# A hybrid attention and convolution layer: mixing of the dilation groups issued in three pieces, its loads ahead of the next chunk's, first two tiles of the output product's left operand split ahead of the last merge

## The chip, the core and the metric

The kernel runs on one core of a Trainium2 chip. Its engines have queues of their own and meet at semaphores: TensorE (PE in the profile, its weight loads PEld), VectorE (DVE), ScalarE (ACT), GpSimd (POOL) and SyncE (SP, which here only issues loads). The metric is the device time of one execution in microseconds, the median over several.

## What is computed

One decoder layer over 2048 tokens and 1024 features, in f32. Cut to what matters here:

```python
proj = h @ w_in + b_in                       # q, k, v | z_attn | u_x, g_b, g_c | z_conv | g_A, g_B
for g, (window, dilation) in enumerate(((128, 1), (512, 4), (2048, 16))):
    o_g, lse_g = dilated_window_attention(q_g, k_g, v_g, window, dilation)
mix_w  = softmax(stack(lse_g), axis=groups)
o_attn = sum over g of mix_w[g] * o_g        # 4 heads of 64: 256 wide
y_attn = (o_attn * silu(z_attn)) @ w_proj_attn
y_conv = (g_b * conv3(g_c * u_x) * silu(z_conv)) @ w_proj_conv
m      = sigmoid(g_A) * y_attn + sigmoid(g_B) * y_conv
x      = layer_norm(alpha * x + gate * (m @ w_out + b_out))
```

Every product of two f32 matrices is made of three: each operand is split into a rounded part (`hi`) and the rest (`lo`), and hi·hi, hi·lo and lo·hi are summed.

## The kernel before

**The input products.** `h @ w_in` is done in 68 groups of two 128-wide tiles of columns over 1024 tokens. A group is done with seven half-size products instead of eight (Strassen), so there are 476 products (`NS`), and `product(n)` works on piece p = n mod 7 of group g = n // 7. One product is 12 matmuls of 128x128 by 512 (lines 1035, 1037, 1038). Four of a group's seven go to the bank `acc[:, g % 2]`, so p = 6 can only start when the result of p = 4 has been taken out of that bank (semaphore `c22_out`). For a group of gates ScalarE takes p = 0, 1, 2 and 6 and VectorE takes p = 3, 4 and 5 (`take_gate`, rows `room<-acc,part`). The gates, made in halves of the tokens, are the last groups of this phase.

**The order on each engine is written out by hand.** Every engine's program is a loop over slots m, one slot for a product. In slot m VectorE takes the result of product m-1 (if p is 3 to 5), then forms the sums of weight tiles for coming products (`combine`, rows `s_tmp<-...` and `w_raw<-w_raw`), then splits the weights of product m+3 (`split_w`, rows `w_lo<-...`), then does whatever else is due in that slot. An engine does its work strictly in that order, and a wait holds all that stands behind it.

**Mixing.** `mix(u)` makes one 128 x 512 piece of `o_attn * silu(z_attn)`: u = 2·chunk + p, for four chunks of 512 tokens and two halves p of the width. For each dilation group dg it waits for that group's data (`mixa_in[dg]`) and multiplies by the weights, for dg 1 and 2 it adds to the first; then one multiplication with `z`, one cast (line 1775) and one subtraction: six multiplications and additions, a cast and a subtraction, all 128x512. `mix(0)` and `mix(1)` stand in slots 452 and 462 of the products (`MIX_AT = NS-24, NS-14`); the other six stand in the merge loop. `load_mix(u, dg)` on SP loads the data of one group: one load of `att_d` (line 681; for dg 2 in runs of 32 elements, 128 bytes) and two of `wg_d` (line 684), for dg 0 also one of `za_d`.

**The merge loop.** After the products come 32 units n = 8·chunk + i, one 128-wide tile of m each. TensorE does `project_att(n)` (6 matmuls, lines 1141 to 1143) and `project_conv(n)` (24 matmuls, lines 1161 to 1163). VectorE does `gate_att(n)` (first gate times attention), in the first chunk `split_wp(n+2)` (rest of a weight tile of `w_proj_conv`, which ScalarE has rounded in `round_wp`, line 1351), at i = 2 and 5 `mix` for the next chunk, at i = 4 and 6 `split_b` (rest of the next chunk's half kh of the convolution's output), and last `merge(n)` (second gate times convolution, then the sum), whose result goes to `mix_d`. SP's part of this loop: `load_merge(n+2)` (the two gates, line 703), at i = 0 `load_b(chunk+1, 0)` and `load_b(chunk+1, 1)` (1 MB each, line 715), at i = 0 and 3 the three groups of a `load_mix`. ScalarE rounds `b` at i = 3 and 5 (`round_b`, line 1347), in the first chunk between the `round_wp`.

**The output product.** Last come 16 tiles of 128 tokens, 48 matmuls each (lines 1203 to 1205). `load_m` brings a tile of m back, `round_m` (ScalarE, line 1437) rounds it and `split_m` (VectorE) makes its rest. TensorE waits for that split (`m_lo_done`), for tile 0 also for the merges of unit 29 and before, for tile 1 for all 32. VectorE's small operations are recorded under line 1459 whatever they do, so its rows are told apart by their tiles.

Of the kernel before, what the change touches and what calls it, by code (L numbers as in the profile page):

```python
# [8 lines left out]
ALU = mybir.AluOpType  # L9
# [156 lines left out]
def build(nc, x, c, w_ada, b_ada, w_in, b_in, conv_w, w_pa, w_pc, w_out, b_out, ln_g, ln_b, out):  # L166
# [23 lines left out]
    with ExitStack() as top:  # L190
# [357 lines left out]
        with nc.Block() as block:  # L548
            @block.sync
            def _(sp):  # L550
# [227 lines left out]
                for n in range(NMU):  # L778
                    chunk, i = unit(n)
                    if n + 2 < NMU:  # L780
                        load_merge(n + 2)
                    if i == 0 and chunk < 3:
                        for kh in range(2):
                            load_b(chunk + 1, kh)
                    for p in range(KA):
                        if i == 3 * p and chunk < 3:
                            for dg in range(3):
                                load_mix(KA * (chunk + 1) + p, dg)
                    for b in range(4):
                        if n == 3 * KT + (0, 1, 3, 5)[b]:  # L790
                            load_wo(b)
                    if n == 3 * KT + 2:
                        load_m(0)
                        load_m(1)
                    if n == 3 * KT + 4:
                        load_xr(0)
                        load_xr(1)
                        load_xr(2)
                        sp.wait_ge(ada_out, 16)
                        sp.dma_start(gb, b_out.broadcast_to([P, D])).then_inc(bc_in, 16)  # L800
                        sp.dma_start(xr[:, 3], ada_d.broadcast_to([P, D])).then_inc(bc_in, 16)
# [650 lines left out]
            def _(dve):  # L1452
# [297 lines left out]
                    dve.wait_ge(pa_rounded, k + 1)  # L1750
                    tt_op(pa_lo[:, k], pa_raw[:, k], pa_hi[:, k].bitcast(F32), ALU.subtract).then_inc(pa_split, 1)

                def mix(u):
                    tc, p = u // KA, u % KA
                    o = mix_a[:, 0]
                    for dg in range(3):
                        a, w = mix_a[:, dg], mix_w[:, dg]
                        dve.wait_ge(mixa_in[dg], 48 * (u + 1))
                        if dg == 0:
                            own_t.up(tt_op(o, a, w, ALU.mult))  # L1760
                            own_t.wait()
                        else:
                            own_t.up(tt_op(by_token(w, dg), natural(a, dg), by_token(w, dg), ALU.mult))
                            own_t.wait()
                            own_t.up(tt_op(o, o, w, ALU.add))
                            own_t.wait()
                    dve.wait_ge(za_in, 16 * (u + 1))
                    own_t.up(tt_op(o, o, mix_z, ALU.mult))
                    own_t.wait()
                    if p == 0 and tc >= 2:  # L1770
                        dve.wait_ge(ya_done, KT * (tc - 1))
                    if p == 0 and tc == 1:
                        for r in range(3):
                            dve.wait_ge(gt_out[r], 16 * gate_stores(r))
                    own_t.up(nc.vector.tensor_copy(o_hi[tc % 2][:, p], o))
                    own_t.wait()
                    tt_op(o_lo[tc % 2][:, p], o, o_hi[tc % 2][:, p].bitcast(F32), ALU.subtract).then_inc(mix_done, 1)
# [44 lines left out]
                for m in range(NS + 2):  # L1822
                    if m and m <= NS:
                        g, p = at(m - 1)
                        kind = PLAN[g].kind
                        if p >= 3:
                            dve.wait_ge(prod, m)
                            if p < 6:
                                dve.wait_ge(sums(g, p)[3], g + 1)
                        if kind in "qkv" and 3 <= p < 6:  # L1830
                            take_rows(g, p)
                        if kind == "ug" and p >= 3:
                            take_ug(g, p)
                        if kind == "gz" and p >= 3:
                            take_gz(g, p)
                        if kind == "za" and p >= 3:
                            take_za(g, p)
                        if kind == "gate" and 3 <= p < 6:
                            take_gate(g, p)
                    if m - 1 in ATT_AT[:NSTEP]:  # L1840
                        bias_max(ATT_AT.index(m - 1))
                    if m - 2 in ATT_AT[2:]:
                        take_o(ATT_AT.index(m - 2) - 2)
                    for n, when in enumerate((-4, -3, -2, 0)):
                        if (m - when) % NP == 0 and (m - when) // NP < NG and (n == 3 or m - when):
                            combine((m - when) // NP, n)
                    if m + 3 < NS:
                        split_w(m + 3)
                    if m < 4:
                        if m == 1:  # L1850
                            dve.wait_ge(t1_ready, 1)
                            tt_op(hs[:, 1], hs[:, 2], hs[:, 1], ALU.subtract).then_inc(t1_ready, 1)
                        if m == 3:
                            dve.wait_ge(dumped["b21"], 16)
                            dve.wait_ge(t1_ready, 2)
                            dve.wait_ge(h_ready, 16)
                            tt_op(hs[:, 3], hs[:, 3], hs[:, 0], ALU.subtract).then_inc(t1_ready, 1)
                        first_t_lo(m + 3)
                    for ph in range(1, 3):
                        for p in range(NP):  # L1860
                            if m == FIRST[ph] + T_LO_AT[p]:
                                split_t(ph, p)
                    if m >= 3 and m - 3 < NS:
                        g, p = at(m - 3)
                        if PLAN[g].kind == "za" and 3 <= p < 6:
                            weigh_za(g, p - 3)
                        if PLAN[g].kind == "ug" and p == 6:
                            taps(g)
                    if m - 2 in TURN_AT:
                        pieces(TURN_AT.index(m - 2))  # L1870
                    for k in range(KT):
                        if m == BG2 + 2 * k + 2:
                            gate_row(k)
                        if m == BG2 + 26 + 2 * k + 2:
                            scale_wo(k)
                    for half in range(2):
                        if m == SUM_AT[half] + 1:
                            gate_sum(half)
                    if m == STAT + 1:
                        copy_stats()  # L1880
                    if m == WEIGH:
                        weigh_groups(0)
                    if m == WEIGH + 4:
                        weigh_groups(1)
                    for k in range(KA):
                        if m == PA_AT + 2 * k + 1:
                            split_pa(k)
                    for u in range(KA):
                        if m == MIX_AT[u]:
                            mix(u)  # L1890
                    for kh in range(2):
                        if m == NS - 2 + kh:
                            split_b(0, kh)
                    for i in range(2):
                        if m == NS + i:
                            split_wp(i)
                for n in range(NMU):
                    c, i = unit(n)
                    gate_att(n)
                    if n + 2 < KT:  # L1900
                        split_wp(n + 2)
                    for kh in range(2):
                        if c < 3 and i == 4 + 2 * kh:
                            split_b(c + 1, kh)
                    for p in range(KA):
                        if c < 3 and i == 2 + 3 * p:
                            mix(KA * (c + 1) + p)
                    for b in range(4):
                        if n == 3 * KT + (2, 3, 5, 7)[b]:
                            split_wo(b)  # L1910
                    merge(n)

                def split_m(tt):
                    r = tt % 2
                    dve.wait_ge(m_hi_done, tt + 1)
                    tt_op(m_part(t_lo, r), m_raw(r), m_part(t_hi, r).bitcast(F32), ALU.subtract).then_inc(m_lo_done, 1)

                split_m(0)
                split_m(1)
                own_t.up(nc.vector.memset(eps[:], LN_EPS))  # L1920
                dve.wait_ge(bc_in, 64)
                own_t.up(tt_op(gb, gb, xr[:, 3], ALU.mult))
# [57 lines left out]
```

## Time and profile before

| | us |
|---|---|
| median of 3 runs | 1983.62 |
| lowest and highest | 1981.62, 1984.23 |
| the profiled execution | 1979.5 |
| its span, first to last instruction | 1977.7 |
| TensorE busy in it | 1907.7 (96%) |
| VectorE busy | 1227.0 (62%) |
| ScalarE busy | 860.7 (44%) |

The span is the time between the first and the last instruction; 1.8 us of the execution lie around it. Busy time of an engine says how much it did, not whether anyone waited for it. A row of the timeline gives an engine's operation with its start and length and, in brackets, how long the engine sat idle before it and what ended that. A row with x6 stands for six operations in one go. The granted clock of TensorE is 1.00 at full speed.

### The profile page before, as it was taken

Reading aid. Unit: us, or ns where it says so; the run is one execution under the profiler, and the core shown is the slowest. Engines: PE = TensorE matmul, PEld = TensorE weight load, DVE = VectorE, ACT = ScalarE, POOL = GpSimd, SP = SyncE. Lnnn points to the kernel's source line nnn. Section 1 sums busy time; section 2 is a strip of 40 time slices with the busy share of each in tenths; the row PEclk is TensorE's granted clock in tenths of the full one; section 3 lists DMA queues with packets and bytes.
Section 4 is the critical chain, followed back from the end, with each engine's and each line's share of the span. In section 5 each row is a group of like instructions: output and inputs, shape, how many; then the busy total and the mean of one; then the engine's idle time right before and its main releaser. Section 6 shows DMA issues by size and latency. Waiting matters only on the chain. (4 is left out here: it accounts for less than half of the span.)

```text
span 1977.7 us, 25526 instructions
## 1 busy us (share of the span) xinstructions
PE 1907.7 (96%) x8989; PEld 1517.6 (77%) x8989; DVE 1227.0 (62%) x2171; ACT 860.7 (44%) x1513; POOL 199.3 (10%) x354
## 2 busy tenths in 40 slices
PE   3799999999999999999989999999999999999998
PEld 3588888877777777777767777777787878887886
DVE  5655564446666666665657666666655665555776
ACT  2544543344545454666665455544553510012222
POOL 0012210120000000011210000000011100000000
PEclk9799999999999999999999999999999999999999
DMA  8566653342323222264762322323255688883442
GB/s 310 188 201 196 205 181 116 96 124 81 97 73 92 80 78 79 85 203 149 257 252 86 96 85 80 92 80 106 81 152 151 210 232 229 243 277 124 149 142 92
DMA packets 303789, 289.03 MB, mean 146 GB/s; under 512 B 38356, under 2 KB 255568, under 8 KB 299952
## 3 DMA queue, kind: packets, MB, share of 16 engines
q1 hardware_dynamic: 277712, 200.06, 35.0%
q0 software_dynamic: 25952, 87.35, 12.2%
q8 instruction: 73, 1.20, 0.3%
q14 instruction: 52, 0.43, 0.1%
HBM read 198.97 MB, written 88.38 MB: 145 GB/s over the span
## 5 line engine op out<-in xcount | busy, mean ns | idle before, releaser
L1035 PE MATMUL acc<-t_hi,w_hi 128*128 128x512 f32 x1904 | 761.0, 400 | 23.6 <-DVE room L1459 13.1
L1038 PE MATMUL acc<-t_hi,w_lo 128*128 128x512 f32 x1904 | 744.7, 391 | 0.0
L1037 PE MATMUL acc<-t_lo,w_hi 128*128 128x512 f32 x1904 | 743.9, 391 | 0.0
L1035 PEld LDWEIGHTS acc<-t_hi,w_hi 128*128 128x128 f32 x1904 | 358.6, 188 | 121.8 <-issue 40.1
L1038 PEld LDWEIGHTS acc<-t_hi,w_lo 128*128 128x128 f32 x1904 | 358.8, 188 | 77.7
L1037 PEld LDWEIGHTS acc<-t_lo,w_hi 128*128 128x128 f32 x1904 | 359.3, 189 | 71.3 <-issue 0.5
L1459 DVE TENSOR_TENSOR room<-acc,part 128x512 f32<-128x512 f32 x204 | 140.8, 690 | 216.9 <-PE acc L1038 215.2
L1459 DVE TENSOR_TENSOR room<-room 128x512 f32<-128x512 f32 (+3 forms) x224 | 178.7, 802 | 98.1 <-DMA room<-wg_d 39.5
L1263 ACT ACTIVATE part<-acc,cols 128x512 f32<-128x512 f32 x204 | 140.1, 687 | 222.3 <-PE acc L1038 221.7
L1459 DVE TENSOR_TENSOR w_lo<-w_raw,w_hi 128x512 fp32r<-128x512 f32 x272 | 184.6, 686 | 60.1 <-ACT w_hi L1245 60.1
L1245 ACT CAST w_hi<-w_raw 128x512 fp32r<-128x512 f32 x272 | 167.5, 616 | 89.5 <-PE acc L1038 87.9
L1245 ACT CAST w_hi<-s_tmp 128x512 fp32r<-128x512 f32 x204 | 126.2, 619 | 144.9 <-PE acc L1038 138.9
L1459 DVE TENSOR_TENSOR w_lo<-s_tmp,w_hi 128x512 fp32r<-128x512 f32 x204 | 140.0, 686 | 65.6 <-ACT w_hi L1245 64.0
L1678 DVE CUSTOM_DVE_ANT_0 room<-score,room 128x128 f32<-128x128 f32 (+1 forms) x192 | 62.5, 363 | 108.9 <-PE score L1073 108.1
L900 POOL DMA_DIRECT2D att_d<-room x96 | 51.7, 539 | 734.2 <-DVE room L1688 726.0
L1339 ACT COPY room<-pt_o 128x256 f32<-128x256 f32 (+1 forms) x96 | 47.2, 491 | 134.1 <-PE pt_o L1082 133.0
L1203 PE MATMUL acc<-t_hi 128*128 128x512 f32 x256 | 99.7, 389 | 2.6 <-DVE t_lo L1459 2.6
L1204 PE MATMUL acc<-t_lo,t_hi 128*128 128x512 f32 x256 | 99.6, 389 | 0.0
L1205 PE MATMUL acc<-t_hi,t_lo 128*128 128x512 f32 x256 | 99.6, 389 | 0.0
L1330 ACT ACTIVATE room<-room 128x128 f32<-128x128 f32 (+1 forms) x192 | 87.0, 454 | 22.5 <-DVE room L1682 22.0
L1161 PE MATMUL acc<-t_hi 128*128 128x512 f32 x192 | 74.9, 390 | 2.3 <-DVE t_lo L1459 2.3
L1162 PE MATMUL acc<-t_lo,t_hi 128*128 128x512 f32 x192 | 74.7, 389 | 0.0
(205 smaller groups left out, 2024.2 us busy)
## 6 DMA issues: line engine op xcount, KB each, us to landing
w_raw<-in_w_in SPq DMA_DIRECT2D x136, 512.0 KB, 5.2
gate_d<-room POOLq DMA_DIRECT2D x64, 256.0 KB, 2.8
w_raw<-gate_d SPq DMA_DIRECT2D x32, 512.0 KB, 5.2
qk_d<-room POOLq DMA_DIRECT2D x24, 512.0 KB, 4.1
room<-qk_d SPq DMA_DIRECT2D x192, 64.0 KB, 2.1
ada_w<-in_w_ada SPq DMA_DIRECT2D x8, 1024.0 KB, 12.1
room<-in_x SPq DMA_DIRECT2D x32, 256.0 KB, 6.4
t_raw<-tr_d SPq DMA_DIRECT2D x8, 1024.0 KB, 8.1
```

What stands on the lines that cost most here:

```text
L1035: nc.tensor.matmul(to, w_hi[:, s, k], t_hi[:, p, k], start=(first and k == 0), stop=False, skip_group_check=True)
L1037: nc.tensor.matmul(to, w_hi[:, s, k], t_lo[:, p, k], start=False, stop=False, skip_group_check=True)
L1038: mm = nc.tensor.matmul(to, w_lo[:, s, k], t_hi[:, p, k], start=False, stop=(last and k == KH - 1), skip_group_check=True)
L1161: nc.tensor.matmul(to, w_h[:, k], b_h, start=(k == 0), stop=False)
L1162: nc.tensor.matmul(to, w_h[:, k], b_l, start=False, stop=False)
L1203: nc.tensor.matmul(to, m_h[:, k], wo_hi[:, k, w], start=(k == 0), stop=False)
L1204: nc.tensor.matmul(to, m_h[:, k], wo_lo[:, k, w], start=False, stop=False)
L1205: mm = nc.tensor.matmul(to, m_l[:, k], wo_hi[:, k, w], start=False, stop=(k == KT - 1))
L1245: nc.scalar.copy(w_hi[:, n % RING], src).then_inc(hi_done, 1)
L1263: ins = nc.scalar.activation(to, src, ACT.Identity, bias=col(gr.tb if p == 1 else gr.ta))
L1330: ex = nc.scalar.activation(prob[:, h, 0:w], prob[:, h, 0:w], ACT.Exp, bias=all_m[:, t, h, blk:blk + 1], scale=SCALE, accum_out=all_d[:, t ...
L1459: return nc.vector.tensor_tensor(o, a, b, op)
```

## The change

Three things are moved; no operation is added or removed.

1. `mix(0)` and `mix(1)`, so far one block each in one slot, are issued in three pieces, one dilation group in each of three slots in a row (`MIX_AT[u] + dg`). The last piece also has the multiplication with `z`, the cast and the subtraction. The six mixes of the merge loop stay whole.
2. In SP's part of the merge loop the loads of the mix (i = 0) are issued ahead of the two loads of the next chunk's `b`.
3. `split_m(0)` and `split_m(1)` on VectorE, so far behind `merge(31)`, stand ahead of it.

```diff
                     if n + 2 < NMU:
                         load_merge(n + 2)
-                    if i == 0 and chunk < 3:
-                        for kh in range(2):
-                            load_b(chunk + 1, kh)
                     for p in range(KA):
                         if i == 3 * p and chunk < 3:
                             for dg in range(3):
                                 load_mix(KA * (chunk + 1) + p, dg)
+                    if i == 0 and chunk < 3:
+                        for kh in range(2):
+                            load_b(chunk + 1, kh)
...
-                def mix(u):
+                def mix(u, dgs=(0, 1, 2)):
                     tc, p = u // KA, u % KA
                     o = mix_a[:, 0]
-                    for dg in range(3):
+                    for dg in dgs:
...
+                    if dgs[-1] < 2:
+                        return
                     dve.wait_ge(za_in, 16 * (u + 1))
...
                     for u in range(KA):
-                        if m == MIX_AT[u]:
-                            mix(u)
+
+                        for dg in range(3):
+                            if m == MIX_AT[u] + dg:
+                                mix(u, (dg,))
...
                             split_wo(b)
+                    if n == NMU - 1:
+                        split_m(0)
+                        split_m(1)
                     merge(n)
...
-                split_m(0)
-                split_m(1)
```

On VectorE, slots 452 to 455 of the products. `room<-acc,part` takes a product out of its bank, `room<-room` is the mix. Before:

```order
L1459 TENSOR_TENSOR room<-acc,part 128x512
L1459 TENSOR_TENSOR s_tmp<-s_tmp,w_raw 128x512
L1459 TENSOR_TENSOR w_lo<-w_raw,w_hi 128x512
L1459 TENSOR_TENSOR room<-room 128x512 x6
L1775 CAST o_hi_a<-room 128x512
L1459 TENSOR_TENSOR o_lo_a<-room,o_hi_a 128x512
L1459 TENSOR_TENSOR room<-acc,part 128x512
L1459 TENSOR_TENSOR w_raw<-w_raw 128x512
```

The same slots now:

```order
L1459 TENSOR_TENSOR room<-acc,part 128x512
L1459 TENSOR_TENSOR s_tmp<-s_tmp,w_raw 128x512
L1459 TENSOR_TENSOR w_lo<-w_raw,w_hi 128x512
L1459 TENSOR_TENSOR room<-room 128x512
L1459 TENSOR_TENSOR room<-acc,part 128x512
L1459 TENSOR_TENSOR w_raw<-w_raw 128x512
L1459 TENSOR_TENSOR w_lo<-s_tmp,w_hi 128x512
L1459 TENSOR_TENSOR room<-room 128x512 x2
L1459 TENSOR_TENSOR room<-acc,part 128x512
L1459 TENSOR_TENSOR w_lo<-s_tmp,w_hi 128x512
L1459 TENSOR_TENSOR room<-room 128x512 x3
L1777 CAST o_hi_a<-room 128x512
```

The take of slot 453 (the second `room<-acc,part`) had eight operations of the mix ahead of it and now has one.

On SP, unit 0 of the merge loop (`conv_d` is the next chunk's `b`; `att_d`, `wg_d` and `za_d` are the mix's data):

```order
+L681 DMA room<-att_d 128x4x128
+L684 DMA room<-wg_d 64x512 x2
+L688 DMA room<-za_d 128x512
+L681 DMA room<-att_d 128x4x128
+L684 DMA room<-wg_d 64x512 x2
+L681 DMA room<-att_d 128x16x32
+L684 DMA room<-wg_d 64x512 x2
 L715 DMA t_raw<-conv_d 128x4x512
 L715 DMA wl_raw<-conv_d 128x4x512
-L681 DMA room<-att_d 128x4x128
-L684 DMA room<-wg_d 64x512 x2
-L688 DMA room<-za_d 128x512
```

Ten loads of the mix went from behind the two of `b` to ahead of them; the gates' loads of unit 3 and later (line 703) follow both, as before.

On VectorE, the end of the merge loop (`w_raw<-acc,w_raw` and `w_raw<-w_raw` are `merge(31)`, `s_tmp` and `part` hold tiles 0 and 1 of m):

```order
-L1459 TENSOR_TENSOR w_raw<-acc,w_raw 128x512
-L1459 TENSOR_TENSOR w_raw<-w_raw 128x512
 L1459 TENSOR_TENSOR t_lo<-s_tmp,t_hi 128x1024
 L1459 TENSOR_TENSOR t_lo<-part,t_hi 128x1024
-L1920 MEMSET eps 128x1
+L1459 TENSOR_TENSOR w_raw<-acc,w_raw 128x512
+L1459 TENSOR_TENSOR w_raw<-w_raw 128x512
+L1925 MEMSET eps 128x1
```

The two splits no longer stand behind the merge of unit 31, which waits for TensorE's last product of the loop.

## Rows read from the trace of the kernel before

**Rows 1.** The page's first part: busy time, share, instructions of each engine.

```profile
PE 1907.7 (96%) x8989; PEld 1517.6 (77%) x8989; DVE 1227.0 (62%) x2171; ACT 860.7 (44%) x1513; POOL 199.3 (10%) x354
```

**Rows 2.** Waits of TensorE: line, waited for, total us, times, longest.

```profile
PE acc L1203 <- DVE t_lo L1459: 2.6, 1, 2.6
PE acc L1161 <- DVE t_lo L1459: 2.3, 2, 1.7
```

**Rows 3.** Timeline, VectorE and TensorE at mix(0): start, length, operation, [idle before].

```profile
1502.44 5.13 DVE L1459 TENSOR_TENSOR room<-room 128x512 f32<-128x512 f32 x6
...
1505.40 0.39 PE L1038 MATMUL acc<-t_hi,w_lo 128*128 128x512 f32 x1
...
1508.67 0.68 DVE L1459 TENSOR_TENSOR room<-acc,part 128x512 f32<-128x512 f32 x1
...
1509.50 0.47 PE L1035 MATMUL acc<-t_hi,w_hi 128*128 128x512 f32 x1 [3.71 <-DVE room L1459]
```

**Rows 4.** Windows behind that rest: PE, PEld, DVE, ACT, POOL busy, then PEclk.

```profile
1510.27:1513.65 3.38, 3.38 (x10) 2.63 (x9) 1.82 (x3) 0.00 (x0) 0.54 (x1) 0.50 0.20 78
```

**Rows 5.** Timeline, TensorE: where full speed is back.

```profile
1513.92 0.40 PE L1035 MATMUL acc<-t_hi,w_hi 128*128 128x512 f32 x1
```

**Rows 6.** Timeline, TensorE, units 0 to 5 of the merge loop.

```profile
1573.20 0.50 PE L1161 MATMUL acc<-t_hi 128*128 128x512 f32 x1 [0.60 <-DVE t_lo L1459]
...
1607.11 0.39 PE L1143 MATMUL score<-o_hi_a,pa_lo 128*128 128x512 f32 x1
1609.24 0.50 PE L1161 MATMUL acc<-t_hi 128*128 128x512 f32 x1 [1.74 <-DVE t_lo L1459]
```

**Rows 7.** Timeline, VectorE: mix(2) in unit 2, then unit 3.

```profile
1596.21 0.69 DVE L1459 TENSOR_TENSOR room<-room 128x512 f32<-128x512 f32 x1 [7.18 <-DMA room<-wg_d]
1599.19 1.82 DVE L1459 TENSOR_TENSOR room<-room 128x512 f32<-128x512 f32 x2 [2.29 <-DMA room<-wg_d]
...
1606.04 0.68 DVE L1459 TENSOR_TENSOR w_raw<-acc,w_raw 128x512 f32<-128x512 f32 x1
...
1607.37 0.68 DVE L1459 TENSOR_TENSOR w_raw<-xb,w_raw 128x512 f32<-128x512 f32 x1
1607.97 1.22 DVE L1459 TENSOR_TENSOR t_lo<-t_raw,t_hi 128x1024 fp32r<-128x1024 f32 x1
```

**Rows 8.** Timeline, SP's queue, unit 0 of the merge loop: issue start, length.

```profile
1581.01 0.41 SPq L715 DMA_DIRECT2D t_raw<-conv_d  x1
...
1591.53 7.84 SPq L684 DMA_DIRECT2D room<-wg_d  x2
1599.41 8.42 SPq L703 DMA_DIRECT2D w_raw<-gate_d  x3
```

**Rows 9.** One line's loads, issue to landing: first of b (L715).

```profile
DMA to landing us min/median/max: 5.8/8.9/12.9
```

**Rows 10.** The same of the gates' loads (L703).

```profile
DMA to landing us min/median/max: 3.8/5.2/8.6
```

**Rows 11.** Timeline, ScalarE: rounding of b's first half and of tiles 5 and 6.

```profile
1589.25 1.91 ACT L1347 CAST t_hi<-t_raw 128x2048 fp32r<-128x2048 f32 x1 [10.13 <-DMA t_raw<-conv_d]
1591.06 1.99 ACT L1351 CAST t_hi<-t_raw 128x1024 fp32r<-128x1024 f32 x2
```

**Rows 12.** Timeline, ScalarE, TensorE and VectorE at the merge loop's end.

```profile
1785.06 1.05 ACT L1437 CAST t_hi<-part 128x1024 fp32r<-128x1024 f32 x1
...
1787.05 2.28 DVE L1459 TENSOR_TENSOR t_lo<-t_raw,t_hi 128x2048 fp32r<-128x2048 f32 x1
...
1791.38 0.39 PE L1163 MATMUL acc<-w_hi,t_lo 128*128 128x512 f32 x1
1791.81 0.69 DVE L1459 TENSOR_TENSOR w_raw<-acc,w_raw 128x512 f32<-128x512 f32 x1 [2.48 <-PE acc L1163]
...
1793.14 1.22 DVE L1459 TENSOR_TENSOR t_lo<-s_tmp,t_hi 128x1024 fp32r<-128x1024 f32 x1
...
1794.42 0.50 PE L1203 MATMUL acc<-t_hi 128*128 128x512 f32 x1 [2.65 <-DVE t_lo L1459]
```

More of the change, by code:

```diff
@@ L1896, in _, with split_m @@
                             split_wp(i)
+                def split_m(tt):
+                    r = tt % 2
+                    dve.wait_ge(m_hi_done, tt + 1)
+                    tt_op(m_part(t_lo, r), m_raw(r), m_part(t_hi, r).bitcast(F32), ALU.subtract).then_inc(m_lo_done, 1)
                 for n in range(NMU):
@@ L1910, in _ @@
                             split_wo(b)
+                    if n == NMU - 1:
+                        split_m(0)
+                        split_m(1)
                     merge(n)
[L1913 to L1916, printed above, removed]
-                split_m(0)
-                split_m(1)
                 own_t.up(nc.vector.memset(eps[:], LN_EPS))
```

## The prediction

> **What bounds the kernel now.** TensorE does. The page's busy shares say so first: it is busy for 1907.7 of the 1977.7 us, VectorE for 62% [rows 1]. So only two things can make the kernel faster: fewer or shorter matmuls, and the change touches none, or fewer rests of TensorE. I therefore read next who TensorE waits for, and then the timeline at each rest behind 1500 us, where the change acts. There are four. Two stand in the waits under lines 1161 and 1203 with VectorE's splits as what ended them [rows 2], of which line 1161 has two; the fourth stands in the middle of the last products, and a take out of a bank ended it [rows 3]. The measure for a rest is the distance from the last start before it to the first behind it, less one ordinary step. That step comes from units 0 to 5: 150 starts (24, then four times 30, then 6) from 1573.20 to 1607.11, 33.91 / 149 = 0.227 us [rows 6].
>
> **Part 1, mix(0) and mix(1) in three pieces.** Before, VectorE enters mix(0) at 1502.44 and comes to the take of the next product at 1508.67: 6.23 us in one block [rows 3]. That product's bank is wanted by p = 6 of the same group. TensorE has started its last ready matmul at 1505.40 and goes on at 1509.50 [rows 3]. The clock then adds to it: from 1510.27 to 1513.65 the granted clock is 0.50, the 1.2 GHz level, after it had been 1.00 through the busy stretch before the rest; from 1513.92 the rows have their usual length again [rows 4, 5]. From the start at 1505.40 to that at 1513.92 there are 8.52 us and 13 steps (to three starts ahead of 1510.27, nine in the slow window, which one more matmul reaches into, and the last); at 0.227 they would take 2.95. This rest and its slow stretch cost 5.57 us.
>
> What is there in its place? One piece is one multiplication, about 0.7 us (the first row of mix(2) has 0.69), the second a multiplication and an addition, 1.82 us [rows 7]; the third is what is left of the block, 6.23 - 0.69 - 1.82 = 3.7 us. In the new order I walk VectorE on: piece 0 from 1502.44 to 1503.1; the product that is to be taken ended at about 1503.1 (12 steps of 0.227, or 2.72, ahead of the end of the next at 1505.8), so the take ends at 1503.9, about 1.9 us before TensorE wants the bank. Then a sum of weights and a split (0.7 each, as all 128x512 operations here) to 1505.2, piece 1 to 1507.0, take and split to 1508.5, piece 2 to 1512.2, then the two operations of slot 455 to 1513.6. The first that is late next would be that split, for product 458, which TensorE starts at 1505.8 + 4 x 2.72 = 16.7, so 3.1 us to spare; and the take of p = 5 (done at 1507.8) is wanted only by the second product of the next group at 1511.2. So the new waits behind the pieces are covered by TensorE's own run, and were the cover gone each us of it would be a us of TensorE. Of mix(1) the change can give back nothing: it stands at p = 0 to 2, where VectorE has no take to do, and no rest there is among TensorE's waits. It costs nothing for the same reason. mix(1)'s data can only be asked for when mix(0) is done, now some 3.5 us later, but that load stands in SP's queue six slots (16 us) behind slot 452. Term: **-5.6 us**, between -5.6 and -3.9 (the 4.10 - 0.23 of the rest alone, if the slow clock comes anyway); the second rival has what a new rest would leave of it.
>
> The trace shows the slow clock behind the rest of 4.10 us and none behind those of 2.13 and 3.04 us, where the step is the usual one at once. The Trainium skill ("TensorE: Matmul & The Clock Gate", Part 1: The HAM clock gate) says that a gate halves the clock once the array has been idle long enough and frees it after sustained work; by that rule the slow stretch goes with the rest that brought it, which gives -5.6 for this term, and without it the sum would have -3.9. The trace agrees as far as one slow stretch can show it.
>
> **Part 2, loads of the mix ahead of those of b.** TensorE stands from 1607.11 to 1609.24 before unit 5's convolution, 2.13 - 0.23 = **1.9 us**, waiting for the rest of weight tile 5 [rows 6]. VectorE makes it at 1607.97, behind mix(2), merge(2) (1606.04) and the gate of unit 3 (1607.37); and mix(2) was late because its data came late: 7.18 and 2.29 us idle before its first two pieces [rows 7]. SP issued b's two loads, 2 MB, at 1581.01, and the mix's behind them [rows 8]. In the new order the mix's first data have no b ahead. How much earlier? Nearest rows: the first of b, issued at 1581.01, lands 8.2 us later by its row's place (ScalarE takes it up at 1589.25 [rows 11]); a load issued there now is the mix's, so VectorE, which comes to mix(2) at about 1589.0 (1596.21 - 7.18), would find dg 0 at 1590 to 1592 rather than 1596.2, and mix(2) ends 4 to 6 us earlier. That is more than the 1.9 that is missing.
>
> But the gates' load of unit 3 stays last in line. It was issued at 1599.41, after a 7.84 us issue of two small `wg_d` loads behind the 128-byte runs of dg 2 [rows 8]; SP has the same issues to do in the new order, so I leave it at 1599.4 at the latest. By its row such a load takes 3.8 to 8.6 us, median 5.2 [rows 10], so it lands at 1603.2 to 1608.0, and now b's 2 MB stand right ahead of it. The chain behind it, gate of unit 3 and split of tile 5, is 1607.97 + 1.22 - 1607.37 = 1.82 us [rows 7]; TensorE wants it at 1607.34. So the rest goes wholly if the gates land by 1605.5, which the median does (1604.6). Term: -1.9 us, between -1.9 and +0.7 (landing at 1608.0: 1609.8 against 1609.2). I take -1.9 since the median is on that side and SP may well be there earlier.
>
> On that: the rows say that the queue stalls for 7.2 to 7.8 us where 128-byte runs are in it. The Trainium skill ("DMA: Bandwidth & Descriptors", Why small descriptors are slow (HBM only)) gives small descriptors a fixed cost each; it speaks against the new order, since all of b and the gates of unit 3 now stand behind such a load. By it the second term would be about 0 and the whole sum -8.4.
>
> b itself now lands later: issued at up to 1598.3 instead of 1581, 5.8 to 12.9 us to landing [rows 9], so 1604 to 1611. Its own use is far off (unit 8, at 1573.2 + 8 x 6.8 = 1628). What stands behind it on ScalarE is the rounding of weight tiles 6 and 7; this is the new wait and a rival below. In chunks 1 and 2 the same exchange takes place; there VectorE idles for the mix's data but TensorE has no rest, and ScalarE has no weight tiles behind b: nothing.
>
> **Part 3, the two splits ahead of merge(31).** TensorE starts its last matmul of the loop at 1791.38 and the first of the output product at 1794.42: 3.04 - 0.23 = **2.8 us**. VectorE idles 2.48 us, until 1791.81, for TensorE's end, does the merge's two operations, and only then, at 1793.14, the split that TensorE waits for [rows 12]. Its inputs had been rounded by 1786.11 (1785.06 + 1.05 for the second). In the new order VectorE is free at 1789.33 (1787.05 + 2.28); two splits at 1.2 bring it to 1791.7, still before it can merge, and TensorE goes on without a rest: tile 0 wants only the merges up to unit 29, and tile 1 comes 48 steps, 10.9 us, later. The splits lie wholly in VectorE's idle 2.48 us; without that cover the merge alone would be later, which is 10 us from being wanted. Term: -2.8 us; if the splits came only behind TensorE's end all the same, just the merge's two operations would go from ahead of them, 1793.14 - 1791.81 = 1.3 us, the other end., lower bound -2.3 should the merge's bank still be waited for in some way that I don't see.
>
> The fourth rest, 0.99 us before 1573.20, stays: nothing of its chain is moved.
>
> **Sum.** -5.6 - 1.9 - 2.8 = -10.3 us. On the profiled execution 1979.5 becomes 1969.2. That execution was 4.1 us below the median of the runs shown, 1983.62, and the rests are a matter of order, not of that offset: 1983.6 - 10.3 = **1973.3 us**.
>
> **The rivals.**
> First, the second rest stays because the gates of unit 3 now come last behind b: -8.4, or **1975.2**. For it: 2 MB more right ahead of them; against: the median landing and a shorter stall when SP's queue starts the mix without b in it. As low as -7.7 if they land at 1608.0.
>
> Second, the pieces don't free TensorE: a take or split behind piece 2, the longest, is late for a product, and the first rest comes back in part, 1.5 to 4 us of the 5.6, with or without the slow clock. Against it are the 1.9 and 3.1 us to spare worked out above; for it, that ScalarE's rounding of slot 456 waits for a sum of slot 455 that stands behind piece 2. Sum -4.3 on the mean: **1979.3**, half of it on either side of 1979.7.
>
> Third, slower: b's first half now comes late to ScalarE, which waits for it in unit 3 and rounds tile 6 only then. From its landing T it is 1.91 + 1.0 + 1.22 + some 0.2 = 4.3 us until TensorE may start unit 6's convolution [rows 7, 11], which it wants at 1607.34 + 6.8 = 1614.1. TensorE stands as soon as T is beyond 1609.8, and everything gained is lost beyond T = 1620.1. The latest by the rows is 1611.2, a rest of 1.4 us; to be slower by 0.2% it would have to be 1624, with a load of 26 us where the longest was 12.9. Price then some 15 us of rest: **1988**.
>
> **How the numbers follow.** Forecast 0.58, first rival 0.27, second 0.12, third 0.03. A measurement of this kernel can tell about 0.2%, 4 us, from no change, so faster means below 1979.7: 0.58 + 0.27 and half of 0.12 is 0.91, of which I leave 0.01 to no change for the runs' own spread of 2.6 us: 0.90. Same: 0.07. Slower: 0.03. Range: downward the forecast less 1.5 us for the medians' spread and less the 0.99 us rest, should it go too, and a little over: 1970.0. Upward the first rival (1975.2) with the clock's 1.7 us not gained and 1.5 us of spread, 1978.4; the other end of the third term lies in it too. That leaves out most of the second and the third.
>
> **What would show it.** Right: TensorE's waits have no row with the take `room` behind 1500 us and none at line 1203; PEclk has no 0.5 in the last products; mix(2)'s first piece starts at about 1591 less 5.6, and TensorE's last matmul before the output product and the first of it are 0.23 us apart. Wrong in part 2: a rest under line 1161 with VectorE's split, VectorE idle for `gate_d` before it. The second rival: a rest in line 1035 ended by `w_lo` or `room` within 15 us of slot 452. The third: a rest under line 1161 of over 3 us while ScalarE waits for `conv_d`. The whole would be wrong if TensorE were slower at its own matmuls, a step other than 0.227.

## The result and the profile after

| | before | changed |
|---|---|---|
| median, us | 1981.61 (6 runs) | 1968.04 (6 runs) |
| lowest and highest | 1981.24, 1984.23 | 1967.17, 1970.05 |
| profiled execution | 1979.5 | 1967.78 |
| its span | 1977.7 | 1965.9 |

The ratio is 0.9931, with a 95% interval from 0.9919 to 0.9942: 13.6 us faster, between 11.5 and 16.1. The forecast was 10.3 us faster and 1973.3, with a range from 1970.0: the direction was right and each of the three rests went, the gain was a third larger, and the time fell out of the range by 2 us.

TensorE's waits in the changed kernel, the lines that answer to [rows 2] (waited for, total us, times, longest):

```profile
PE acc L1035 <- DVE room L1459: 9.4, 3, 5.5
...
PE acc L1161 <- DVE t_lo L1459: 0.6, 1, 0.6
```

There is no row of line 1203 any more, line 1161 has kept only the rest of 0.6 us that the prediction left alone, and of the four waits for `room` that line 1035 had before (13.1 us together), the one of 3.7 us is gone. The windows around the three places (columns as in [rows 4]):

```profile
1490.00:1510.00 20.00, 20.00 (x90) 16.57 (x89) 12.86 (x19) 10.10 (x17) 2.43 (x5) 1.00 0.35 112
1590.00:1610.00 20.00, 20.00 (x90) 16.57 (x89) 15.44 (x19) 5.62 (x4) 1.62 (x3) 1.00 1.06 283
1775.00:1795.00 20.00, 20.00 (x90) 16.57 (x89) 11.30 (x12) 3.46 (x4) 1.08 (x2) 1.00 0.55 158
```

TensorE is busy for all of each 20 us, at a granted clock of 1.00, where before there were rests and a stretch at 0.50.

VectorE at the pieces of mix(0), which answers to [rows 3] (timeline):

```profile
1501.31 0.69 DVE L1459 TENSOR_TENSOR room<-room 128x512 f32<-128x512 f32 x1
1502.04 0.69 DVE L1459 TENSOR_TENSOR room<-acc,part 128x512 f32<-128x512 f32 x1
...
1504.08 1.82 DVE L1459 TENSOR_TENSOR room<-room 128x512 f32<-128x512 f32 x2
1505.93 0.69 DVE L1459 TENSOR_TENSOR room<-acc,part 128x512 f32<-128x512 f32 x1
```

The take that TensorE waits for starts 0.73 us behind the start of the mix, not 6.23.

VectorE at mix(2) and unit 3, which answers to [rows 7]:

```profile
1582.22 0.68 DVE L1459 TENSOR_TENSOR room<-room 128x512 f32<-128x512 f32 x1
1584.67 1.81 DVE L1459 TENSOR_TENSOR room<-room 128x512 f32<-128x512 f32 x2 [1.76 <-DMA room<-wg_d]
1588.01 2.56 DVE L1459 TENSOR_TENSOR room<-room 128x512 f32<-128x512 f32 x3 [1.53 <-DMA room<-wg_d]
...
1595.83 0.69 DVE L1459 TENSOR_TENSOR w_raw<-xb,w_raw 128x512 f32<-128x512 f32 x1 [2.73 <-DMA w_raw<-gate_d]
1596.43 1.22 DVE L1459 TENSOR_TENSOR t_lo<-t_raw,t_hi 128x1024 fp32r<-128x1024 f32 x1
```

The first piece no longer waits at all (7.18 us before), and the gates of unit 3 are now what comes last, as the first rival had it: VectorE idles 2.73 us for them. But it is done with the split at 1597.65 and TensorE starts unit 5's convolution at 1600.61, so that wait costs nothing. SP's queue there, which answers to [rows 8]:

```profile
1573.68 0.60 SPq L681 DMA_DIRECT2D room<-att_d  x1
...
1578.94 5.69 SPq L684 DMA_DIRECT2D room<-wg_d  x2
1584.72 1.36 SPq L715 DMA_DIRECT2D t_raw<-conv_d  x1
...
1586.69 6.79 SPq L703 DMA_DIRECT2D w_raw<-gate_d  x3
```

From the first load of the group to the gates' it is 13.0 us, where it was 18.4: the long issue behind the 128-byte runs is 5.69 instead of 7.84, and the shorter ones ahead of it shrank too.

The end of the merge loop, which answers to [rows 12]:

```profile
1780.49 1.22 DVE L1459 TENSOR_TENSOR t_lo<-s_tmp,t_hi 128x1024 fp32r<-128x1024 f32 x1
...
1782.62 0.39 PE L1163 MATMUL acc<-w_hi,t_lo 128*128 128x512 f32 x1
1782.85 0.39 PE L1203 MATMUL acc<-t_hi 128*128 128x512 f32 x1
...
1783.05 0.69 DVE L1459 TENSOR_TENSOR w_raw<-acc,w_raw 128x512 f32<-128x512 f32 x1 [0.21 <-PE acc L1163]
```

The output product starts 0.23 us behind the last start of the loop, one ordinary step, and the two splits lie in what was VectorE's idle time.

**What the two traces leave open.** I matched the starts of TensorE's matmuls in both traces, one by one. The changed kernel gains 5.5 us around mix(0), 2.0 at unit 5 and 2.9 at the output product, 10.4 together, so the sum of 10.3 is right on this pair. It is 1.15 us ahead before the first changed instruction: a wait for a load at 881 us (1.2) is gone. That is no work of the change, since only the first trace of the kernel before has this wait and the twelve others of this study don't. It makes 11.6 of the spans' 11.8. The medians say 13.6. Two theories: (A) the slow clock follows TensorE's rests in some executions and not in others, and the profile of before showed an execution with little of it; (B) the surplus lies elsewhere, in waits for loads.

### The profile page after: what moved, and what is told of

Its sections match the earlier page's. It is cut to its first block, busy times and chain, and to the rows that moved or that the text cites. A ratio compares the mean times of both kernels' runs of the same rounds, so it can differ in the third digit from the quotient of the medians.

```text
span 1965.9 us, 25526 instructions
## 1 busy us (share of the span) xinstructions
PE 1906.4 (97%) x8989; PEld 1518.2 (77%) x8989; DVE 1227.8 (62%) x2171; ACT 860.7 (44%) x1513; POOL 199.3 (10%) x354
## 3 DMA queue, kind: packets, MB, share of 16 engines
q0 software_dynamic: 25952, 87.35, 12.3%
## 4 chain that ended last, share of the span: by engine, by line
PE 92%; DVE 2%; DMA 2%; ACT 2%; issue 1%; SPq 0%; DVEq 0%; ACTq 0%
PE acc L1035 22%; PE acc L1038 21%; PE acc L1037 21%; PE acc L1161 3%; PE acc L1205 3%; PE acc L1163 3%; PE acc L1204 3%; PE acc L1162 3%; PE acc L1203 3%; PE score L1073 3%; PE pt_o L1082 2%; PE xb L1105 2%; DMA ada_w<-in_w_ada 1%; PE xb L1108 1%; DVE room L1459 1%
## 5 line engine op out<-in xcount | busy, mean ns | idle before, releaser
L1204 PE MATMUL acc<-t_lo,t_hi 128*128 128x512 f32 x256 | 99.6, 389 | 0.0
L1205 PE MATMUL acc<-t_hi,t_lo 128*128 128x512 f32 x256 | 99.6, 389 | 0.0
L1163 PE MATMUL acc<-t_hi,t_lo 128*128 128x512 f32 x192 | 74.7, 389 | 0.0
```

What stands on the lines that cost most here:

```text
L1163: mm = nc.tensor.matmul(to, w_l[:, k], b_h, start=False, stop=(k == KT - 1))
L1204: nc.tensor.matmul(to, m_h[:, k], wo_lo[:, k, w], start=False, stop=False)
L1205: mm = nc.tensor.matmul(to, m_l[:, k], wo_hi[:, k, w], start=False, stop=(k == KT - 1))
```

## The experiments

Each was timed in five rounds beside the kernel before, and has a trace. A stretch at half clock was found as steps of 0.427 us between starts of 512-column matmuls, where 0.227 is the ordinary one.

**The kernel before again** (no edit).

> The kernel before, unchanged, for its own spread. In its first profile TensorE had the slow clock behind one of the three rests only (4.10 us) and its profiled execution, 1979.5 us, was faster than all six timed ones (1981.24 to 1984.23). Theory A (the granted clock is what the trace of one execution missed: in most executions one or two more rests bring a slow stretch of 1.6 to 1.7 us each): median 1981 to 1983, and the second profile, if it is 1.6 us or more longer than 1979.5, shows one stretch at 0.50 more. Theory B (executions differ elsewhere, in waits for DMA ahead of 1500 us): the same medians, but a longer profile shows longer waits for loads and the same slow stretches.

Measured: 1981.89 (12 runs, 1977.61 to 1985.56), ratio 1.0003 (0.9992 to 1.0014). The profiled execution took 1977.61, 2 us less than the first profile though it shows a stretch at 0.50 more, behind a rest of 2.9 us at 1025 us that all these kernels have. It had shorter waits for loads, as (B) has it, 1.2 us at 881 and 0.8 at 1274: between two single traces (B) is real. Two windows of that trace (columns as above):

```profile
1026.00:1029.50 3.50, 3.50 (x10) 2.71 (x9) 2.05 (x4) 0.04 (x1) 0.54 (x1) 0.52 1.01 413
1508.50:1510.60 2.10, 2.10 (x6) 1.65 (x5) 1.95 (x4) 0.01 (x1) 0.54 (x1) 0.50 0.32 125
```

The slow stretch behind mix(0) is 2.1 us here and was 3.4 [rows 4]; that behind the rest at 1025 was not there at all in the first trace. So a single trace doesn't tell what a rest costs. Nor does every slow stretch cost time. Behind 1025 us the first trace, without one, has a second rest, ended by a take of ScalarE, and the nine traces with a slow stretch there have 0.8 us of idle or less in its place (the first trace, then the changed kernel's):

```profile
1036.78 0.47 PE L1035 MATMUL acc<-t_hi,w_hi 128*128 128x512 f32 x1 [2.07 <-ACT part L1263]
```

```profile
1035.88 0.47 PE L1035 MATMUL acc<-t_hi,w_hi 128*128 128x512 f32 x1 [0.42 <-ACT part L1263]
```

From 1015 to 1060 us none of the nine loses or gains more than 0.3 us on the first trace: there the slow matmuls only fill time that TensorE would have waited.

With the executions' mean granted clock beside the time, the 69 timed ones of the kernel before (of this and the later calls) fall into

| mean granted clock | executions | median us |
|---|---|---|
| 0.991 | 10 | 1978.2 |
| 0.990 | 23 | 1980.9 |
| 0.989 | 22 | 1982.2 |
| 0.988 | 12 | 1983.4 |
| 0.987 | 2 | 1983.8 |

Half clock for x us lowers the mean by x/2/1980, and takes x/2 us of work away if TensorE is busy all the while, so a step of 0.001 is at most 2.0 us; the table has 5.2 us over three steps. So the clock goes with a good part of this kernel's spread (correlation -0.75), not with all: at 0.990 alone the times reach from 1977.62 to 1983.17.

**Each part alone.** The edits are the three pieces of the diff: the pieces, the order of SP's loads, the place of the splits.

> Only mix(0) and mix(1) in three pieces; loads and last splits as before. Forecast: the rest of 4.10 us in the last products and its slow stretch go, -5.6 us, and the rests before unit 5 (1.9) and before the output product (2.8) stay. Theory A: -5.6 to -6.5. Theory B: -5.6 plus or minus 1. If the pieces alone give -7.5 or more, the surplus of the whole change lies here.

Measured: 1975.03 (6 runs), ratio 0.9969 (0.9958 to 0.9980), 6.1 us faster, between 4.0 and 8.3.

> Only the mix's loads ahead of b's. Forecast: the rest before unit 5 goes, -1.9 us; first rival of the prediction: it stays, 0. Theory A (slow clock behind this rest in many executions of before): -1.9 to -3.6. Theory B: -1.9 plus or minus 1. The trace tells when the gates of unit 3 land and when VectorE comes to the split of tile 5 (before: 1607.97).

Measured: 1977.32 (11 runs), ratio 0.9981 (0.9972 to 0.9989), 3.8 us faster, between 2.2 and 5.5.

> Only the splits of tiles 0 and 1 of m ahead of the last merge. Forecast: the rest before the output product goes, -2.8 us. Theory A (slow clock behind this rest in many executions of before): -2.8 to -4.5. Theory B: -2.8 plus or minus 1.

Measured: 1976.02 (8 runs), ratio 0.9974 (0.9964 to 0.9984), 5.2 us faster, between 3.2 and 7.1.

Each part gains at least its rest, and the three add up to 15.1, which the intervals don't tell from 13.6. The second and third lie above what their rests are worth without the clock (1.9 and 2.8), both with the whole of their intervals. The traces show a reason for the third. With the pieces alone, the two rests that stay both have the slow clock behind them (timeline, then windows around what follows):

```profile
1602.20 0.79 PE L1161 MATMUL acc<-t_hi 128*128 128x512 f32 x1 [2.72 <-DVE t_lo L1459]
```

```profile
1602.50:1605.50 3.00, 3.00 (x8) 2.36 (x8) 2.97 (x5) 0.00 (x0) 0.54 (x1) 0.55 0.92 300
1789.50:1793.00 3.50, 3.50 (x10) 2.69 (x10) 2.71 (x4) 0.00 (x0) 0.00 (x0) 0.51 0.80 202
```

And with the order alone, behind the rest before the output product:

```profile
1789.30:1792.30 3.00, 3.00 (x9) 2.32 (x8) 2.85 (x4) 0.00 (x0) 0.00 (x0) 0.50 0.88 235
```

In the trace of before neither place had it. The first of these rows shows something else: with the pieces alone the rest before unit 5 grew, from 1.74 to 2.72 us of idle. TensorE comes there 8.0 us earlier than before, the split only 7.0, because VectorE's waits for mix(2)'s data grew by 1.0 us (7.87, 2.92 and 1.01 now, 7.18, 2.29 and 1.35 before).

Why the second part gives 3.8 us and not 1.9 stays open. The mean granted clock rose with it (0.9902, where the kernel before had 0.9895 beside it), and the rest before unit 5 differs from execution to execution; but in the three traces of kernels with `mix(0)` in one block in slot 452 and b's loads first, where this rest is not filled, it is 1.5 to 2.1 us long, with no slow stretch behind it. That it is longer in other executions is not shown.

**The rests filled.** The kernel before in its own order; where TensorE rested it now multiplies data that nobody reads, into banks that are free:

```diff
+                def fill(to, count, x):
+                    for _ in range(count):
+                        nc.tensor.matmul(to, x[:, 0:P], x, start=True, stop=True, skip_group_check=True)
...
+                    if n == MIX_AT[0] + 2:
+                        pe.wait_ge(max_ready, NSTEP)
+                        fill(sc_ps[:, 0], 15, t_hi[:, 0, 0])
...
+                    if n == 5:
+                        pe.wait_ge(att_gated, 3)
+                        fill(po[:], 8, t_hi[:, 1, 0])
...
+                    if tt == 0:
+                        pe.wait_ge(att_gated, NMU - 3)
+                        fill(sc_ps[:, 0], 11, t_hi[:, 6, 0])
```

> The kernel before, in its own order, with matmuls that nobody reads put where TensorE rested: 15 of 128x512 (3.4 us) ahead of the product that waits for mix(0), 8 (1.8 us) ahead of unit 5's convolution, 11 (2.5 us) ahead of the output product. The waits last as long as before, so the 8.6 us of rests stay lost. Theory A (the surplus of the change over 10.3 us is slow clock that follows these rests in many executions, not in all): no stretch at 0.50 behind 1400 us in the trace, and 3 to 5 us faster than before. Theory B (the surplus lies elsewhere, in waits for DMA): no faster than before, rather slower by up to 0.5 us per filling that overruns its wait.

Measured: 1977.19 (11 runs), ratio 0.9981 (0.9972 to 0.9990), 3.7 us faster, between 2.0 and 5.5, with 34 matmuls more and every wait as long as before. Its timeline at mix(0) and the window around it:

```profile
1502.77 3.56 PE L1008 MATMUL score<-t_hi 128*128 128x512 f32 x15
1506.59 0.50 PE L1042 MATMUL acc<-t_hi,w_hi 128*128 128x512 f32 x1 [0.26 <-DVE room L1472]
```

```profile
1500.00:1520.00 20.00, 19.74 (x87) 15.98 (x87) 12.95 (x19) 7.84 (x13) 2.16 (x4) 1.00 0.22 75
```

The product starts no sooner than it did (4.04 us between useful starts, 4.10 before; 2.04 and 3.04 at the other two, 2.13 and 3.04 before), yet no stretch at 0.50 is left behind 1400 us while TensorE works, and the mean granted clock of the 11 executions is 0.9918, against 0.9894 of the kernel before. This separates the theories for the medians: idle time taken from TensorE alone, with nothing else moved, gives 3.7 us. That is (A), and (B) gives no reason for it. It also says what the clock is worth here: by the mean clock alone, 0.0024 of 1980 us, it would have been 4.8 us, and 3.7 were measured. Between single traces (B) still counts: of the 4.6 us that this trace is shorter than the first, 2.9 lie ahead of the first filled rest.

**The order's share beside the other two.** The changed kernel with the loads as before.

```diff
-                    for p in range(KA):
-                        if i == 3 * p and chunk < 3:
-                            for dg in range(3):
-                                load_mix(KA * (chunk + 1) + p, dg)
                     if i == 0 and chunk < 3:
                         for kh in range(2):
                             load_b(chunk + 1, kh)
+                    for p in range(KA):
+                        if i == 3 * p and chunk < 3:
+                            for dg in range(3):
+                                load_mix(KA * (chunk + 1) + p, dg)
```

> The changed kernel with the loads in their old order (parts 1 and 3 alone). In the run of part 1 alone the rest before unit 5 had grown from 2.13 to about 3.0 us, because TensorE comes to unit 5 earlier and VectorE, held by loads, does not. So in place of the forecast's 1.9 us the order is worth 2.8 us plus the slow clock that may follow: this kernel 2.8 to 4.5 us slower than the changed one, 1971 to 1972.5; by the forecast's terms alone 1.9 slower, 1970.

Measured: 1971.33 (5 runs, 1967.76 to 1972.10), ratio 0.9949 (0.9937 to 0.9962): 3.3 us slower than the changed kernel's median. The profiled execution is the fastest of them, and its rest before unit 5 is 0.89 us from start to start instead of 2.13 or 3.11:

```profile
1600.58 0.50 PE L1161 MATMUL acc<-t_hi 128*128 128x512 f32 x1 [0.49 <-DVE t_lo L1459]
```

So this rest has no fixed length: here VectorE's waits for mix(2)'s data are 9.6 us together, with the pieces alone they were 11.8. The median fits the expectation, the trace of one execution alone would not have.

**The block in another slot.**

```diff
-MIX_AT = (NS - 24, NS - 14)
+MIX_AT = (NS - 20, NS - 14)
```

> The kernel before with mix(0) still in one block, but in slot 456 instead of 452, where VectorE has no product to take for three slots (as mix(1) has in slot 462). If it is the take behind the block that TensorE waits for, the whole of part 1 is had: no rest there, -5.6 to -6.5 us against before, as e1_pieces. If the length of the block holds up the splits of weights too, a rest of up to 3 us remains under line 1035 behind slot 456.

Measured: 1981.04 (11 runs), ratio 1.0003 (0.9994 to 1.0011): nothing gained. A miss. The rest at mix(0) did go; a rest of 4.16 us came at mix(1), and the one before unit 5 grew to 3.36. VectorE and TensorE there:

```profile
1529.57 0.69 DVE L1459 TENSOR_TENSOR room<-room 128x512 f32<-128x512 f32 x1 [1.79 <-DMA room<-wg_d]
1533.47 1.81 DVE L1459 TENSOR_TENSOR room<-room 128x512 f32<-128x512 f32 x2 [3.20 <-DMA room<-wg_d]
1536.74 2.51 DVE L1459 TENSOR_TENSOR room<-room 128x512 f32<-128x512 f32 x3 [1.46 <-DMA room<-wg_d]
```

```profile
1541.10 0.79 PE L1035 MATMUL acc<-t_hi,w_hi 128*128 128x512 f32 x1 [3.77 <-DVE w_lo L1459]
```

mix(1)'s loads wait for mix(0) to be done, which now was at 1518.3; its data came late, and VectorE, idle for them 6.45 us in the middle of the block, had the splits of weights behind it. So the chain from mix(0) over its buffers to mix(1)'s data is close to the limit, and here a block that waited for its loads cost as much as the long one that it replaced.

**One block more from in front of a take.** On the changed kernel:

```diff
-T_LO_AT = tuple(x + 1 for x in T_HI_AT)
+T_LO_AT = (-5, -4, -1, 1, 2, 3, 4)
```

> The changed kernel with one more block taken from in front of a take: at the start of the second phase of products VectorE's split of the third tile of h (2.3 us) stands in slot 298, ahead of the take of p = 4; here in slot 300 behind the take of p = 5. TensorE rests 2.95 us there (start to start) and five of six traces have a slow stretch behind it. Expected: that rest goes, 2.7 us and some 1.2 us of slow clock, 3 to 4.5 us faster than the changed kernel: 1964 to 1965. Rival: the rest moves to the next take, since VectorE has four such splits to do in these slots anyway, and nothing or 1 us is gained.

Measured: 1967.36 (5 runs), ratio 0.9932 (0.9920 to 0.9945): as the changed kernel, and not 3 to 4.5 us faster. The rest of 2.95 us went to 0.75, and another came:

```profile
1034.97 0.47 PE L1035 MATMUL acc<-t_hi,w_hi 128*128 128x512 f32 x1 [4.34 <-ACT part L1263]
```

ScalarE had idled until 1030.45 for a gate's store, and TensorE, earlier now, ran into it. The rival was right in kind, wrong in who is late next.

**The store's wait taken away.** ScalarE's fourth result of a gate group goes to a room of its own (`tmp3`), so that it need not wait for the store of the first.

```diff
-                        act.wait_ge(gt_out[0], 16 * (2 * done + 1))
-                        nc.scalar.activation(tmp[:, 0], src, ACT.Sigmoid, bias=col(gr.tb)).then_inc(c21_act, 1)
+                        act.wait_ge(gt_out[0], 16 * 2 * done)
+                        nc.scalar.activation(tmp3, src, ACT.Sigmoid, bias=col(gr.tb)).then_inc(c21_act, 1)
```

> The changed kernel, unchanged, for its own spread and beside the other two of this call. 1967 to 1969, mean granted clock 0.992, no stretch at 0.50 behind 1400 us.

Measured: 1967.50 (5 runs), ratio 0.9923 (0.9910 to 0.9935).

> The changed kernel, where ScalarE writes the fourth result of a gate group to a room of its own and no longer waits until the first result of the same group, in the room that both used, has been stored (5.4 us idle at 1031 in the changed kernel's trace). TensorE's rest at 1025, which VectorE's splits bring, stays: theory (the two waits lie one behind the other): 0 to 1 us faster than the changed kernel.

Measured: 1962.47 (4 runs), ratio 0.9899 (0.9885 to 0.9912): 5.0 us faster than the changed kernel beside it, not 0 to 1.

> e9_gate_room and the later split of e6_split_t together. In e6_split_t TensorE's rest of 2.95 us went and one of 4.73 us came eight us later, ended by ScalarE, which had idled 5.97 us for the store of a gate. Theory: with both waits gone that rest goes as well, up to 4 us and its slow clock: 3 to 5 us faster than the changed kernel, 1963 to 1965. Rival: VectorE's four splits of 2.3 us are then late for the next take, and 1 us or less is gained.

Measured: 1960.42 (4 runs), ratio 0.9886 (0.9871 to 0.9901): 7.1 us faster than the changed kernel, 22.8 faster than the one before. ScalarE at that place in the changed kernel and, in the second fence, with its own room:

```profile
1031.35 0.69 ACT L1272 ACTIVATE room<-acc,cols 128x512 f32<-128x512 f32 x1 [5.35 <-DMA gate_d<-room]
```

```profile
1026.40 0.69 ACT L1272 ACTIVATE room<-acc,cols 128x512 f32<-128x512 f32 x1 [2.46 <-PE acc L1038]
```

Both forecasts were too low (0 to 1 and 3 to 5 us). That of the store's wait alone looked at one wait only. The edit takes the wait out of every gate group; the changed kernel's trace has five of them, 19.8 us of ScalarE's idle time together, and one lies ahead of TensorE's rest at 1025:

```profile
1005.76 0.69 ACT L1272 ACTIVATE room<-acc,cols 128x512 f32<-128x512 f32 x1 [5.92 <-DMA gate_d<-room]
```

With it gone ScalarE rounds VectorE's next inputs earlier, and VectorE's split of the tile of h starts at 1011.52 instead of 1013.58. TensorE's rest from VectorE's splits is 2.07 us, where it was 2.95; the three rests ended by ScalarE's takes there (1.8 us together beyond a step) went, and neither execution's trace has a slow stretch there. Between 1007 and 1060 us TensorE gains 5.1 us, nearly all that the traces differ by. With the later split besides, the rest of 2.07 is gone, and TensorE's waits on line 1035 for `room` are two from VectorE and one from ScalarE:

```profile
PE acc L1035 <- ACT room L1224: 7.8, 1, 7.8
PE acc L1035 <- DVE room L1459: 6.8, 2, 5.6
```

## Why the prediction was wrong where it was

**What bounds the kernel, and what ends the three rests**: right. Each of the three rests went, each part alone gained, and VectorE's walk through the pieces fits the trace within 0.1 us (take 0.73 us behind the start of the mix, second take 4.62; 0.7 and 4.6 in the working).

**Part 2**: right in the result. The term of the data's arrival was too careful: mix(2)'s first data were there before VectorE, where 1 to 3 us of wait were forecast, because SP's own issues took 5.4 us less without b ahead; I had left the queue's stalls as they were. The first rival's mechanism is in the trace and had 3 us to spare. In the two traces the term is 2.0 us against 1.9; the medians of the order alone give 3.8 (2.2 to 5.5), and the rest of that is open.

**Part 3**: right for the rest, 2.9 us against 2.8 in the two traces; the medians of this part alone give 5.2 (3.2 to 7.1), with the clock in it.

**The step that failed is the clock's.** The prediction let the slow stretch follow the rest of 4.10 us only, and gave the other two none, since the trace showed none "behind those of 2.13 and 3.04 us". That took one execution's trace for all. In the thirteen traces of this study, behind their first 90 us, the slow clock follows the 2.9 us rest at 1025 in nine of ten, the rest of about 4.1 at a mix in four of five, the 3.0 before the output product in two of five, the rest before unit 5 where it was over 3 us in two of two, and the rest of 4.7 us that came with the other split of t in one of one; it follows neither the rest of 2.46 us nor any under 2.2. The sum had 5.57 - 3.87 = 1.7 us of clock. The filled rests give its size: 3.7 us (2.0 to 5.5). With 3.7 in its place the sum is 10.3 + 2.0 = 12.3, and measured were 13.6 (11.5 to 16.1); what is left, 1.3 us, is within the intervals and no run says where it lies. The mean clock, 0.9894 before and 0.9918 after, would give 0.0024 x 1977 = 4.8 us and a sum of 13.4, nearer to the 13.6, but it sizes the clock too high: with the same 0.9918 the filled kernel had gained 3.7.

The Trainium skill ("TensorE: Matmul & The Clock Gate", Part 1: The HAM clock gate) itself says that the point at which the gate changes varies from run to run, since it depends on where in a free-running period the first matmul falls; it says so of the start of a stream of matmuls. I read its rule against the single slow stretch in the trace and not that sentence. The runs agree with it for a rest in the middle too: the rest at mix(0), in the order of before, brought a slow stretch of 3.4 us in one execution [rows 4], of about 2.1 us in two others and none in a fourth (the kernel with the order alone).

**The base**: 1983.62 was the median of three runs. The six runs beside the result give 1981.61 and all 69 give 1981.3. In the time both errors go the same way and add up to 5.3 us (3.3 too small a gain, 2.0 too high a base). With the base right the range would have ended at 1968.0, at the measured 1968.04, so the base alone decided whether the time fell into the range; the gain would still have been a third too small. The range's lower end gave 1.5 us to the medians' spread, 1.0 to a fourth rest and nothing to the clock at the other two.

**The rivals**: the second, a late split behind the pieces, and the third, b late for ScalarE, did not come. The price of the second was wrong in itself: 1.5 to 4 us back is 2.75 on the mean, so -7.5 and 1976.1 us, not -4.3 and 1979.3, and the whole of its 0.12 belonged to "faster". ScalarE had b at 1591.29 and the weight tiles rounded by 1595.1, before it mattered.

## What to carry to other kernels

Where one engine is the bound, list its rests with what ended each; moving the block out of the way of the one instruction that is waited for gives the rest back, if what is late next has been looked up too, loads and stores included (two of the experiments only moved a rest). Cost a rest of TensorE with the clock behind it, and take the chance of that from several executions' traces, since one trace shows one draw; the mean granted clock gives the most that it can cost. A block of work that waits for data is split, or its data asked for earlier, before it is moved.

## What the runs showed of the hardware

Matmuls that nobody reads, put into TensorE's rests, made the kernel 3.7 us faster, with the mean granted clock up from 0.9894 to 0.9918. Behind the first 90 us of the thirteen traces (in which rests and stretches at 0.50 follow each other closely) rests under 2.2 us never had a slow stretch behind them; rests of 2.9 to 4.7 us had one in 18 of 23 cases, from 2.1 to 5.1 us long. One at mix(0) of 3.4 us cost 1.7; one at 1025 us cost at most 0.3, because TensorE would have waited behind it anyway. In unit 0 of the merge loop SP's issue of the two `wg_d` loads behind the load in 128-byte runs took 5.4 to 6.9 us in the six traces with the mix's loads first and 7.4 to 9.2 in the seven with b's first.
